# Expert rows gathered into overlapping neighbours of a ring of 4 KB places

## What is computed

```
q = (xt @ w_query).reshape(T, PEER_HEADS, 2, PEER_HALF)
s = einsum('thsk,snk->thsn', q, sub_keys);  sv, si = top_k(s, 16)
cand = sv[:, :, 0, :, None] + sv[:, :, 1, None, :];  cv, ci = top_k(cand, 16)
idx = i1 * PEER_N_KEYS + i2;  g = softmax(cv)
hid = gelu(einsum('td,thkd->thk', xb, expert_u[ib]))
out = einsum('thk,thkd->td', g * hid, expert_v[ib])
x = x + out
```

## Time and profile before

| | |
|---|---|
| median of 3 timed runs | 4051.21 us (4047.34 to 4053.17) |
| span of the profiled execution (the only time given for it) | 5878.7 us |
| TensorE busy in it | 5726.4 us, 97% |
| VectorE / ScalarE / GpSimd busy | 49% / 28% / 22% |
| moved by DMA | 1444.45 MB, mean 246 GB/s over the span |
| mean granted TensorE clock | 0.555 |

### The profile page before, as it was taken

The page is one execution under the profiler, slowest core; times in us unless marked ns, Lnnn a source line. Parts: engine busy times, 40 slices in busy tenths (PEclk is TensorE's granted clock), DMA queues, the critical chain, the costliest instruction groups (busy, mean ns, idle before and its releaser), DMA issues.

```text
span 5878.7 us, 40315 instructions
## 1 busy us (share of the span) xinstructions
PE 5726.4 (97%) x13374; PEld 2787.7 (47%) x13374; DVE 2887.4 (49%) x5745; ACT 1648.5 (28%) x4216; POOL 1285.3 (22%) x1094
## 2 busy tenths in 40 slices
PE   9999999999999998999999999899999999899999
PEld 5555555444444545444445545344445555222222
DVE  3321003665555455756555555756555554744443
ACT  3431101344422211244432211245422211222222
POOL 0000000222222221322222221322222221334343
PEclk6555555555555555555555555555555555555555
DMA  4222222767777775767777775777777775899997
GB/s 155 93 102 81 73 90 95 267 238 266 261 275 268 274 280 202 285 245 280 273 272 297 283 291 190 280 256 271 271 268 308 281 290 191 315 350 342 345 342 281
DMA packets 212948, 1444.45 MB, mean 246 GB/s; under 512 B 27256, under 2 KB 27256, under 8 KB 46340
## 3 DMA queue, kind: packets, MB, share of 16 engines
q0 software_dynamic: 164976, 1133.94, 52.0%
q1 hardware_dynamic: 47632, 307.80, 14.4%
q10 hardware_dynamic: 132, 0.12, 0.0%
HBM read 1439.31 MB, written 7.13 MB: 246 GB/s over the span
## 4 chain that ended last, share of the span: by engine, by line
PE 96%; DVE 2%; ACT 1%; issue 1%; DMA 0%; SPq 0%; ACTq 0%; DVEq 0%
PE banks L609 52%; PE sums L871 21%; PE banks L871 7%; PE banks L748 5%; PE banks L827 3%; PE banks L669 2%; PE banks L736 1%; PE banks L786 1%; PE banks L778 1%; PE banks L694 1%; PE banks L844 1%; DVE x L1479 1%; DVE rows L1470 0%; PE banks L637 0%; PE banks L700 0%
## 5 line engine op out<-in xcount | busy, mean ns | idle before, releaser
L609 PE MATMUL banks<-hT,ring 128*128 128x256 f32 x6656 | 2608.4, 583 | 4.7 <-DVE arena L1316 3.9
L609 PEld LDWEIGHTS banks<-hT,ring 128*128 128x128 f32 x6656 | 1507.5, 228 | 1151.7 <-issue 734.0
L576 POOL DMA_INDIRECT rows<-in_w_uv,idx x1024 | 1237.6, 1209 | 3600.3 <-PE sums L871 1981.3
L1470 DVE CUSTOM_DVE_ANT_0 rows<-rows,xn 128x1024 f32<-128x1024 f32 x1024 | 1241.6, 1220 | 530.8 <-DMA rows<-in_w_uv,idx 528.0
L871 PE MATMUL sums<-rows,diag 128*128 128x512 f32 x1612 | 1285.2, 970 | 70.0 <-ACT diag L1076 47.9
L1479 DVE SCALAR_TENSOR_TENSOR x<-rows,wgt,x 128x1024 f32<-128x1024 f32 x493 | 632.0, 1282 | 234.8 <-ACT wgt L1068 234.0
L871 PEld LDWEIGHTS sums<-rows,diag 128*128 128x128 f32 x1612 | 369.2, 232 | 791.7 <-issue 683.2
L1281 DVE SCALAR_TENSOR_TENSOR arena<-banks,pr,arena 128x254 f32<-128x254 f32 (+1 forms) x512 | 246.8, 482 | 354.6 <-ACT arena L965 340.9
L1063 ACT ACTIVATE gelu<-hid 128x2 f32<-128x2 f32 x512 | 102.9, 201 | 1100.7 <-DVE hid L1470 1099.3
L609 PE MATMUL banks<-yT,ring 128*128 128x256 f32 x1024 | 400.2, 582 | 0.0
L871 PE MATMUL banks<-rows,diag 128*128 128x512 f32 x512 | 393.7, 966 | 0.0
(11 more groups left out here) (205 smaller groups left out, 2955.8 us busy)
## 6 DMA issues: line engine op xcount, KB each, us to landing
ring<-in_w_ssd SPq DMA_DIRECT2D x96, 1024.0 KB, 5.4
ring<-in_w_att SPq DMA_DIRECT2D x64, 1024.0 KB, 6.1
ring<-in_w_mrg SPq DMA_DIRECT2D x52, 1024.0 KB, 8.4
arena<-a_rows POOLq DMA_DIRECT2D x32, 1024.0 KB, 7.6
ring<-in_w_qry SPq DMA_DIRECT2D x32, 1024.0 KB, 4.8
arena<-bias_tiles POOLq DMA_DIRECT2D x16, 1152.0 KB, 7.3
ring<-in_w_out SPq DMA_DIRECT2D x16, 1024.0 KB, 7.0
rows<-in_w_uv,idx POOLq DMA_INDIRECT x1024, 6.8
```

Of the source, the lines that this page charges most:

```text
L576: nc.gpsimd.indirect_dma_start(out=rows[n % NB][:, :], out_offset=None, in_=w_uv, in_offset=bass.IndirectOffsetOnAxis(ap=idx[:, t, s:s + 1 ...
L609: mm = pe.matmul(out, w[:, k * P:(k + 1) * P], rhs[:, k0 + k, :], start=start and k == 0, stop=stop and k == n - 1)
L1470: v.tensor_tensor_reduce(u, u, xn2[:, (n // SLOTS_T) % 3, :], 1.0, 0.0, ALU.mult, ALU.add, hid[:, k:k + 1]).then_inc(u_done, 1)
```

## The change

The 8 buffers become a ring of 17 places of 4 KB (and one more behind the last). Gather n lands in place n * 12 mod 17 (its u half) and the next one (its v half). With these numbers the v half of gather n lies where the u half of gather n - 7 lay, and its u half where the v half of gather n - 10 lay. So gather n waits for the dot product of step n - 7 and for the sum of step n - 10, and it is asked for six steps ahead. There are ten landing semaphores in place of eight.

The room comes from smaller buffers: `xn2` has two tiles (three before), `idx` and `gate` two (four before), `hid`, `gelu` and `wgt` 16 columns (256 before). Since tile 1 of `xn2` is still read by the steps of the pass before, it is written later, in group 1 of the next pass's ssd stage, from a kept copy of its scale. The norm weights are loaded twice per pass, straight into the `xn2` tile that is then scaled in place.

```diff
-NB = 8
 LAG = 3
-AHEAD = NB - LAG - 1
+AHEAD = 6
+U_AGAIN = AHEAD + 1
+V_AGAIN = AHEAD + LAG + 1
+PLACES = U_AGAIN + V_AGAIN
+STEP = pow(V_AGAIN, -1, PLACES)
+HID = 16
...
-        xn2 = sb("xn2", [P, 3, D])
+        xn2 = sb("xn2", [P, 2, D])
...
-        rows = [sb(f"rows{n}", [P, 2 * D]) for n in range(NB)]
+        rows_all = sb("rows", [P, (PLACES + 1) * D])
+
+        def row_of(n):
+
+            first = n * STEP % PLACES
+            return rows_all[:, first * D:(first + 2) * D]
...
+                if m:
+                    yield place("ssd", 0, 0.3)
+                    late_norm_rows(m - 1)
                 yield place("ssd", 0, 0.5)
...
-                yield place("norm2", 0, 0.2)
-                pool.wait_ge(x_mid.sem, x_mid.at(m, 2))
-                pool.dma_start(n2b, w_n2[m // 2].partition_broadcast(P)).then_inc(n2_in.sem, 16)
+                yield place("out", 0, 0.2)
+                if m:
+                    pool.wait_ge(u_done, SLOTS_P * (m - 1) + SLOTS_T)
+                norm_rows(m, 0)
+
+            def norm_rows(m, t):
+
+                pool.dma_start(xn2[:, t, :], w_n2[m // 2].partition_broadcast(P)).then_inc(n2_in.sem, 16)
+
+            def late_norm_rows(m):
+
+                if m:
+                    pool.wait_ge(u_done, SLOTS_P * m)
+                norm_rows(m, 1)
...
-                if n >= NB:
-                    summed(pool, n - NB)
+                if n >= U_AGAIN:
+                    pool.wait_ge(u_done, n - U_AGAIN + 1)
+                if n >= V_AGAIN:
+                    summed(pool, n - V_AGAIN)
                 nc.gpsimd.indirect_dma_start(
-                    out=rows[n % NB][:, :], out_offset=None, in_=w_uv,
-                    in_offset=bass.IndirectOffsetOnAxis(ap=idx[:, t, s:s + 1], axis=0)).then_inc(g_in[n % NB], 16)
+                    out=row_of(n), out_offset=None, in_=w_uv,
+                    in_offset=bass.IndirectOffsetOnAxis(ap=idx[:, t, s:s + 1], axis=0)).then_inc(g_in[n % V_AGAIN], 16)
...
+            def rows_of(m, t, scale):
+
+                v.wait_ge(n2_in.sem, n2_in.at(m, 16 * (t + 1)))
+                v.scalar_tensor_tensor(out=xn2[:, t, :], in0=x[:, 2 * (m % 2) + t, :], scalar=scale, in1=xn2[:, t, :],
+                                       op0=ALU.mult, op1=ALU.mult).then_inc(xn_ok.sem, 1)
+
+            def late_rows(m):
+
+                v.wait_ge(keep_ok, m + 1)
+                rows_of(m, 1, stat[:, 32:33])
...
+                        if m and g == 1:
+                            late_rows(m - 1)
...
-                v.wait_ge(n2_in.sem, n2_in.at(m, 16))
-                for t in range(2):
-                    if m:
-                        v.wait_ge(u_done, SLOTS_P * (m - 1) + SLOTS_T)
-                    v.scalar_tensor_tensor(out=xn2[:, (2 * m + t) % 3, :], in0=x[:, 2 * b + t, :], scalar=stat[:, 12 + t:13 + t], in1=n2b,
-                                           op0=ALU.mult, op1=ALU.mult).then_inc(xn_ok.sem, 1)
+                rows_of(m, 0, stat[:, 12:13])
+                v.tensor_copy(stat[:, 32:33], stat[:, 13:14]).then_inc(keep_ok, 1)
...
-                v.wait_ge(g_in[n % NB], 16 * (n // NB + 1))
-                u = rows[n % NB][:, 0:D]
-                v.tensor_tensor_reduce(u, u, xn2[:, (n // SLOTS_T) % 3, :], 1.0, 0.0, ALU.mult, ALU.add, hid[:, k:k + 1]).then_inc(u_done, 1)
+                v.wait_ge(g_in[n % V_AGAIN], 16 * (n // V_AGAIN + 1))
+                u = row_of(n)[:, 0:D]
+                v.tensor_tensor_reduce(u, u, xn2[:, k // SLOTS_T, :], 1.0, 0.0, ALU.mult, ALU.add, hid[:, k % HID:k % HID + 1]).then_inc(u_done, 1)
...
+                if k == 4:
+                    late_rows(PASSES - 1)
```

More of the change, by code:

```diff
@@ L286, in build @@
         rstdB = sb("rstdB", [P, SEQ])
-        xn2 = sb("xn2", [P, 3, D])
[L288 to L292, removed]
+        xn2 = sb("xn2", [P, 2, D])
+        idx = sb("idx", [P, 2, SLOTS_T], U32)
+        gate = sb("gate", [P, 2, SLOTS_T])
+        hid = sb("hid", [P, HID])
+        gelu = sb("gelu", [P, HID])
+        wgt = sb("wgt", [P, HID])
         diag = [sb(f"diag{n}", [P, P]) for n in range(DIAGS)]
-        rows = [sb(f"rows{n}", [P, 2 * D]) for n in range(NB)]
+        rows_all = sb("rows", [P, (PLACES + 1) * D])
+        def row_of(n):
+            first = n * STEP % PLACES
+            return rows_all[:, first * D:(first + 2) * D]
         late_keys = sb("late_keys", [P, 4 * SLOTS_T])
@@ L327, in build @@
         junk = cut(D)
-        n2b = cut(D)
-        after_n = used[0]
-        first = rows[NB - 1]
+        first = row_of(AHEAD)
         rel_w, hot_rel, mask_rel, row_rel = first[:, 3 * RW:3 * RW + NG * 8], first[:, 0:RW], first[:, RW:2 * RW], first[:, 2 * RW:3 * RW]
@@ L445, in build @@
         sg_ok, m_v, mT_ok = count("sg_ok", 16), count("m_v", 24), count("mT_ok", 8)
-        out_mm, x_mid, n2_in = count("out_mm", 1), count("x_mid", 2), count("n2_in", 16)
+        out_mm, x_mid, n2_in = count("out_mm", 1), count("x_mid", 2), count("n2_in", 32)
         q_ev, q_s, q_sv = count("q_ev", 16), count("q_s", PH), count("q_sv", PH)
-        k_v, i_ok, s_d, s_e, s_v2 = (sem(n) for n in ("k_v", "i_ok", "s_d", "s_e", "s_v2"))
+        k_v, i_ok, s_d, s_e, s_v2, keep_ok = (sem(n) for n in ("k_v", "i_ok", "s_d", "s_e", "s_v2", "keep_ok"))
         xn_ok = count("xn_ok", 2)
-        g_in = [sem(f"g_in{n}") for n in range(NB)]
+        g_in = [sem(f"g_in{n}") for n in range(V_AGAIN)]
         u_done, g_ge, g_w, d_ok, v_pe, v_dve = (sem(n) for n in ("u_done", "g_ge", "g_w", "d_ok", "v_pe", "v_dve"))
@@ L589, in _ @@
             together(mixer, tick)
-            pool.wait_ge(xn_ok.sem, xn_ok.at(PASSES, 0))
+            late_norm_rows(PASSES - 1)
+            pool.wait_ge(xn_ok.sem, xn_ok.at(PASSES - 1, 1))
             pool.dma_start(wfin, w_final.partition_broadcast(P)).then_inc(f_w, 16)
@@ L871, in tick @@
                         mm = pe.matmul(sum_banks(p, t)[:, h, :], diag[e % DIAGS][:, :],
-                                       rows[n % NB][:, D + 512 * h:D + 512 * h + 512], start=q == mine[0], stop=q == mine[-1])
+                                       row_of(n)[:, D + 512 * h:D + 512 * h + 512], start=q == mine[0], stop=q == mine[-1])
                     mm.then_inc(v_pe, 1)
@@ L1060, in tick @@
                 n = p * SLOTS_P + k
-                t = 2 * (p % 2) + k // SLOTS_T
+                t = k // SLOTS_T
+                c = (n - 1) % HID
                 act.wait_ge(u_done, n + 1)
-                act.activation(gelu[:, k - 1:k + 1], hid[:, k - 1:k + 1], ACT.Gelu).then_inc(g_ge, 1)
+                act.activation(gelu[:, c:c + 2], hid[:, c:c + 2], ACT.Gelu).then_inc(g_ge, 1)
                 act.wait_ge(g_ge, n // 2 + 1)
@@ L1067, in tick @@
                 for q in (k - 1, k):
-                    act.activation(wgt[:, q:q + 1], gelu[:, q:q + 1], ACT.Copy,
+                    h = q % HID
+                    act.activation(wgt[:, h:h + 1], gelu[:, h:h + 1], ACT.Copy,
                                    scale=gate[:, t, q % SLOTS_T:q % SLOTS_T + 1]).then_inc(g_w, 1)
@@ L1075, in tick @@
                             act.wait_ge(v_pe, e - DIAGS + 1)
-                        act.activation(diag[e % DIAGS][:, :], ident, ACT.Copy, scale=wgt[:, q:q + 1]).then_inc(d_ok, 1)
+                        act.activation(diag[e % DIAGS][:, :], ident, ACT.Copy, scale=wgt[:, q % HID:q % HID + 1]).then_inc(d_ok, 1)
             def final(s, t):
@@ L1199, in route @@
                     link(v.tensor_scalar(row[t][:, ks], idh[t][:, 0, ks], float(P), float(l * EXPERTS), ALU.mult, ALU.add))
-                    v.tensor_tensor(idx[:, 2 * b + t, ks], row[t][:, ks], idh[t][:, 1, ks], ALU.add).then_inc(i_ok, 1)
+                    v.tensor_tensor(idx[:, t, ks], row[t][:, ks], idh[t][:, 1, ks], ALU.add).then_inc(i_ok, 1)
                     if n:
@@ L1478, in tick @@
                         v.wait_ge(v_dve, dve_sums(p, q) - 1)
-                    v.scalar_tensor_tensor(out=xo, in0=rows[before % NB][:, D:], scalar=wgt[:, q:q + 1], in1=xo,
+                    v.scalar_tensor_tensor(out=xo, in0=row_of(before)[:, D:], scalar=wgt[:, q % HID:q % HID + 1], in1=xo,
                                            op0=ALU.mult, op1=ALU.add).then_inc(v_dve, 1)
```

8 lines of the change are left out of this document (4 added, 4 removed).

## The result

The changed kernel takes 4057.16 us in the median of 20 runs (4052.13 to 4064.45), the kernel before 4050.97 in 20. The ratio is 1.0017, with an interval of 1.0010 to 1.0023: 7 us slower (4 to 9), where 54 us less were forecast. One run of the kernel before, far out at 12646.76 us, does not count in the ratio.

The account below looks back on a forecast made before the run. The prediction took transfers to bound the timed runs, with TensorE the bound under the profiler. From 4051 us it took 60 for deeper gathers, added 5 for norm loads and 1 for a copy: 3997 us, range 3890 to 4070.

Parts of the forecast that it names:

- Clock: Whole kernel: the timed runs were taken to have full clock, though the profiled execution was granted 0.55 to 0.57.
- The bound: Timed runs: transfers bound, with floors of 3766 or 3883 us, leaving 168 to 285 us of DMA idle to reach.
- The sign that I named: Middle passes at full clock: they would run above 390 GB/s, with the last stretch unchanged.
- The four under way before cover 9.9 us ... six cover 14.9: Longer stalls, four per pass over three passes: each leaves up to 5.0 us less DMA idle, 60 us gained.
- the end of a pass: Counted as one stall of each pass; the first gather's wait for its index there was not counted as a gain.
- The pair buffers hid, gelu, wgt of 16 columns: The smaller buffers, with two-tile idx and gate: new waits only on work one pass old, 0 us.
- Doubled norm load: Norm weights loaded twice per pass: 2.1 MB more, 5 us at 423 GB/s if transfers bound.
- The late write, the copy, the second wait per gather: Tile 1 scaled in the next pass: hidden; one column copied: 1 us; two waits per gather: no added lead needed.
- The last 251 steps: The end, gathers alone: already saturated with five under way, so 0 gain and 3.1 us per step kept.
- B: Rival, chance 0.26: two gathers cover every stall and TensorE holds its clock, so timed runs fall to 3945 to 3889 us.
- C: Rival, chance 0.22: TensorE or VectorE's chain of waits bounds the timed runs, not transfers; no gain, some 4054 us.
- D: Rival, chance 0.12: weight tiles land late behind six queued gathers; 52 loads each 2 us late give 4161 us.

Follow-up runs that it names:

- a_ahead4_aligned: The changed kernel with AHEAD = 4 (13 places) and 64 unused bytes ahead of its ring of places: 4068.98 us, ratio 1.0038 to the kernel before.
- b_copy: The kernel before, unchanged, run again for a profile at the clock of the timed runs; its median in the experiments' rounds was 4050.8 to 4055.2 us.
- a_aligned: The changed kernel with 64 unused bytes ahead of its ring, which then starts at a multiple of 256 bytes: 4031.94 us, ratio 0.9949 to the kernel before.

## Why the prediction was wrong, point by point

- **Clock.** Right in the main: full clock in the timed runs was inferred from two times, and the profiles of both kernels at 0.94, nearly full, have spans within 2.5 us of the medians.
- **The bound.** Right that transfers bound, wrong in how much was idle. I took 423 GB/s (427 it is), "reached with four under way" (3.2 on the mean of those ten microseconds), and read all above the floor, 168 to 285 us, as idle DMA engines. At 0.96 busy the three middle passes have about 0.05 x 2720 = 136 us of idle against the 1.01 of a full stretch. The rest is packets that are slower beside the mixer: 390 / 0.96 = 406 GB/s per full share against 427 / 1.01 = 423 (an 8 KB packet of a gather took 321 ns there before, and 309 in the stretch of gathers alone). What slows them was not tried. The sign that I named, over 390 GB/s in the middle passes, tells nothing: it is 389 to 392 after and was 387 to 392 before.
- **"The four under way before cover 9.9 us ... six cover 14.9", at four stalls per pass: this step failed, 60 us where the runs show 27.** The gain is 7 - 28 - 6 = -27 us, the measured +7 with the two costs below taken off. AHEAD is the step in which the gather is written down, not how many are under way; GpSimd runs ahead of that to its waits. In the middle passes, where the stalls are, these let 3.2 be under way on the mean before and 3.9 to 4.0 after, less than one more in place of two. Only in the last stretch, where more depth was rightly priced at 0, did it rise from 5.2 to 6.4. The four stalls per pass were a choice, and one of them, the end of a pass, gives nothing: 352 GB/s before and 355 after over 320 us. The steps named as dealt at 3.5 to 3.9 us aren't all: by the table out and norm2 have 2.8 and query 6.3. Where in the passes the 27 us are won was not located.
- **A term that was missing: +28 us.** The smaller buffers moved the start of the places by 64 bytes from a multiple of 256. This step failed too, and it is the one that turned the sign: "The pair buffers hid, gelu, wgt of 16 columns" stood at 0, priced by their waits alone. With the 64 bytes it takes 4031.94 us.
- **Doubled norm load.** Forecast 5, measured 6 (intervals just overlap). Right.
- **The late write, the copy, the second wait per gather.** Forecast 1 us together; not taken apart, but they are within the 27.
- **The last 251 steps.** Forecast unchanged, with five under way; 5.2 were. Right about depth, 427 GB/s with and without it, wrong by the layout: 5 of 427 GB/s over 610 us are 7 of the 28 us.
- **Rivals.** B's mechanism is not there: TensorE's clock is 0.942 after and 0.944 before. C's number (4054) came closest by luck: 6 KB gathers show that transfers bound, and a gain of 27 us was cancelled by 28 + 6. D did not occur: the landing of the state-space weights is 8.8 us after and 8.4 before, that of the attention weights 9.1 in both, and no wait of TensorE in either profile was ended by a load of the ring.

## What to carry to other kernels

Before pricing deeper prefetch, count what is really under way, stretch by stretch: time to landing divided by the time from one transfer to the next. If the DMA engines are over 95% busy, one more under way can still smooth (about 40 us or 1% here), but a change of the layout by 64 bytes weighs nearly as much as this change gained. When a change resizes any buffer, look up where the transfers' targets now start, and compare GB/s at equal DMA share in a stretch that holds nothing else.

## What the runs showed of the hardware

- 8 KB writes that start 192 bytes past a multiple of 256 took 1.5% longer per packet than those at a multiple (315 against 310 ns; 421 or 422 against 427 GB/s with full engines), in both kernels. 128 bytes past, for weight loads, made no difference to the time (4031.26 us with them at a multiple, 4031.94 without).
- Indirect gathers of 128 rows of 8 KB kept the 16 DMA engines full at 426 or 427 GB/s over 400 us, with 4.3 (a_ahead4_aligned), 5.2 (b_copy) and 6.4 (a_aligned) of them under way on the mean.
- The kernel before ran at a granted clock of 0.555 throughout one profiled execution, 5878.7 us, and at 0.944 in another, 4048.8 us. What sets this was not found.
